# Gate and up products of eight feed-forward turns as two 64-row halves of TensorE's array, the halves changing PSUM banks

## What is computed

```python
h = rms_norm(x, norm2_g[l])
x = x + (jax.nn.silu(h @ w_gate[l]) * (h @ w_up[l])) @ w_down[l]
```

## Time and profile before

| | |
|---|---|
| median of 2 runs | 1517.21 us (1516.51 to 1517.91) |
| profiled execution, its own time | 1516.28 us |
| its span in the profile | 1514.5 us |
| TensorE's mean granted clock in it | 0.998 of full |
| PE, PEld, DVE, ACT busy | 99%, 85%, 71%, 53% of the span |
| DMA | 268.21 MB, mean 177 GB/s |

### The profile page before, as it was taken

How to read it: one execution, slowest core, us unless ns; L and a number is a source line. 1 busy time by engine, 2 the same in 40 slices (tenths; PEclk the granted TensorE clock), 3 DMA queues, 4 the chain that set the end, 5 groups by cost and what they waited for, 6 DMA issues and landing times.

```text
span 1514.5 us, 19707 instructions
## 1 busy us (share of the span) xinstructions
PE 1504.1 (99%) x8062; PEld 1281.8 (85%) x8062; DVE 1072.1 (71%) x1354; ACT 798.4 (53%) x950; POOL 46.6 (3%) x52
## 2 busy tenths in 40 slices
PE   9999999999999999999999999999999999999997
PEld 7888888888888888888888888888888888888886
DVE  5778666676786666885767786666877657876666
ACT  6646444456464444665445364444665455454444
POOL 0100000001000000000300100000002000000000
PEclk9999999999999999999999999999999999999999
DMA  9534545554346555445344455554535445455551
GB/s 295 218 111 174 216 179 200 185 188 167 109 171 217 173 198 181 162 177 175 142 158 165 169 194 197 193 193 174 183 120 197 146 165 181 167 209 194 191 198 56
DMA packets 47802, 268.21 MB, mean 177 GB/s; under 512 B 8288, under 2 KB 11744, under 8 KB 17888
## 3 DMA queue, kind: packets, MB, share of 16 engines
q1 hardware_dynamic: 44960, 264.92, 49.4%
q10 hardware_dynamic: 2752, 2.03, 0.4%
HBM read 262.99 MB, written 1.05 MB: 174 GB/s over the span
## 4 chain that ended last, share of the span: by engine, by line
PE 99%; DVE 0%; DMA 0%; SPq 0%; issue 0%; DVEq 0%; ACT 0%
PE psum L670 21%; PE psum L574 19%; PE psum L576 19%; PE psum L575 19%; PE psum L679 11%; PE psum L612 4%; PE psum L981 1%; PE psum L999 1%; PE psum L1066 1%; PE psum L1075 1%; PE psum L840 0%; PE psum L824 0%; PE psum L988 0%; DMA x<-in_x 0%; PE psum L1053 0%; PE psum L843 0%
## 5 line engine op out<-in xcount | busy, mean ns | idle before, releaser
L1596 DVE TENSOR_TENSOR wl<-raw,wh 128x2048 fp32r<-128x2048 f32 (+1 forms) x247 | 554.7, 2248 | 221.2 <-ACT wh L1176 221.1
L1176 ACT ACTIVATE wh<-raw 128x2048 fp32r<-128x2048 f32 (+2 forms) x249 | 465.9, 1874 | 323.1 <-PE psum L576 200.5
L574 PE MATMUL psum<-wh,xhl 128*128 128x512 f32 (+2 forms) x928 | 365.6, 394 | 0.0
L576 PE MATMUL psum<-wh,xhl 128*128 128x512 f32 (+2 forms) x928 | 357.9, 386 | 0.0
L575 PE MATMUL psum<-wl,xhl 128*128 128x512 f32 (+2 forms) x928 | 357.2, 385 | 0.0
L670 PE MATMUL psum<-xhl,wh 128*128 128x512 f32 x1408 | 336.7, 391 | 0.0
L670 PEld LDWEIGHTS psum<-xhl,wh 128*128 128x128 f32 x1408 | 261.3, 188 | 52.3
L574 PEld LDWEIGHTS psum<-wh,xhl 128*128 128x128 f32 x928 | 174.9, 188 | 34.9 <-issue 2.5
L576 PEld LDWEIGHTS psum<-wh,xhl 128*128 128x128 f32 x928 | 174.6, 188 | 34.7
L575 PEld LDWEIGHTS psum<-wl,xhl 128*128 128x128 f32 x928 | 175.1, 189 | 31.9
L679 PEld LDWEIGHTS psum<-xhl,wl 128*128 128x128 f32 x1408 | 175.3, 192 | 3.8
(11 more groups left out here) (208 smaller groups left out, 1185.9 us busy)
## 6 DMA issues: line engine op xcount, KB each, us to landing
raw<-in_weights SPq DMA_DIRECT2D x233, 1024.0 KB, 4.8
raw<-in_weights SPq DMA_DIRECT2D x10, 512.0 KB, 3.7
raw<-in_weights SPq DMA_DIRECT2D x4, 832.0 KB, 4.3
raw<-in_weights SPq DMA_DIRECT2D x12, 256.0 KB, 8.1
raw<-in_weights SPq DMA_DIRECT2D x2, 768.0 KB, 4.1
arena<-arena SPq DMA_DIRECT2D x8, 192.0 KB, 4.6
work<-in_rpb ACTq DMA_DIRECT2D x8, 141.0 KB, 5.7
arena<-work SPq DMA_DIRECT2D x16, 64.0 KB
```

What stands on the lines that cost most here:

```text
L574: nc.tensor.matmul(dst, lh, right(wh, slot), start=start, stop=False)
L576: return nc.tensor.matmul(dst, ll, right(wh, slot), start=False, stop=stop)
L1176: nc.scalar.activation(wh[:, slot, 0:n], raw[:, slot, 0:n], ACT.Copy).then_inc(high_ready.sem, 1)
L1596: nc.vector.tensor_tensor(wl[:, slot, 0:n], raw[:, slot, 0:n], wh[:, slot, 0:n].bitcast(F32), ALU.subtract).then_inc(split_ready.sem, 1)
```

## The change

Turns 2 to 9 call `gate_up_in_rows` in place of `gate_up` (turn 1 and turn 10 keep the old form). Each stationary tile of 128 rows is cut into rows 0 to 63 and rows 64 to 127, and each moving tile likewise, so a product becomes two of 64 rows, issued one after the other. The two halves write two neighbouring banks: in one run of 8 matmuls the lower half works for group `first` and the upper half for group `first + 1`, and in the `swapped` run the other way round, so that each bank gets both halves. Before a half goes to a bank that the other half has written, PE waits for the end of that run by a new semaphore, `turned`, which the last matmul of the run raises. There are eight such waits and eight such signals in a turn. The sums, the banks, the pieces and the programs of ACT, DVE and SP stay as they are.

```diff
+    "turned": (8 * (FFI - 3), 8 * (FFI - 3)), "aq_ready": (0, 1), "ak_ready": (0, 1), "bv_in": (0, 64),
...
+                def gate_up_in_rows(i, q, slot):
+                    n = 8 * (i - 2)
+                    def run(first, swapped, k0, slot, wide):
+                        for kk in range(4):
+                            for half in range(2):
+                                rows = slice(64 * half, 64 * half + 64)
+                                c = first + (half ^ swapped)
+                                place = bank((up_banks(i) if c >= 2 else gate_banks(i)) + c % 2)
+                                right = slice(kk * 512 + c * P, kk * 512 + (c + 1) * P)
+                                if wide:
+                                    mm = nc.tensor.matmul(place, wh[rows, slot, right],
+                                                          xhl[rows, k0 + kk, :, :].rearrange("p a b -> p (a b)"),
+                                                          start=(k0, kk, swapped) == (0, 0, 0),
+                                                          stop=(k0, kk, swapped) == (4, 3, 0), skip_group_check=True)
+                                else:
+                                    mm = nc.tensor.matmul(place[:, 0:SEQ], wl[rows, slot, right], xh[rows, k0 + kk, :],
+                                                          start=False, stop=False, skip_group_check=True)
+                        return mm
+
+                    pe.wait_ge(*split_ready.by(L, q + 1))
+                    for first in (0, 2):
+                        pe.wait_ge(*proj_free[first // 2].by(L, U + i))
+                        run(first, 0, 0, slot, True).then_inc(turned.sem, 1)
+                    for first in (0, 2):
+                        pe.wait_ge(*turned.by(L, n + 1 + first // 2))
+                        run(first, 1, 0, slot, True)
+                    for first in (0, 2):
+                        run(first, 1, 0, slot, False).then_inc(turned.sem, 1)
+                    for first in (0, 2):
+                        pe.wait_ge(*turned.by(L, n + 3 + first // 2))
+                        mm = run(first, 0, 0, slot, False)
+                    mm.then_inc(piece_used.sem, 1)
+
+                    slot = (slot + 1) % RING
+                    pe.wait_ge(*split_ready.by(L, q + 2))
+                    for first in (0, 2):
+                        run(first, 0, 4, slot, False).then_inc(turned.sem, 1)
+                    for first in (0, 2):
+                        pe.wait_ge(*turned.by(L, n + 5 + first // 2))
+                        run(first, 1, 4, slot, False)
+                    for first in (0, 2):
+                        run(first, 1, 4, slot, True).then_inc(turned.sem, 1)
+                    for first in (0, 2):
+                        pe.wait_ge(*turned.by(L, n + 7 + first // 2))
+                        run(first, 0, 4, slot, True).then_inc(piece_used.sem if first else proj_full[0].sem, 1)
...
                 def turn(i, q, start):
-                    gate_up(i, q, (F + 2) % RING)
+                    (gate_up if start else gate_up_in_rows)(i, q, (F + 2) % RING)
                     down(i - 1, q + 2, (F + 4) % RING, start)
```

More of the change, by code:

```diff
@@ L100 @@
     "a_ready": (11, 11), "ah_ready": (11, 11), "al_ready": (11, 11), "end_ready": (1, 1), "end_high": (1, 1), "end_low": (1, 1), "diag_ready": (1, 1), "row_full": (1, 1), "row_ready": (1, 1),
-    "aq_ready": (0, 1), "ak_ready": (0, 1), "bv_in": (0, 64),
+    "turned": (8 * (FFI - 3), 8 * (FFI - 3)), "aq_ready": (0, 1), "ak_ready": (0, 1), "bv_in": (0, 64),
     "s_full": (0, len(TURNS)), "max_ready": (0, len(TURNS)), "p_ready": (0, len(TURNS)),
@@ L322, in build @@
         s_full, max_ready, p_ready = S["s_full"], S["max_ready"], S["p_ready"]
-        unit_ready, bv_in = S["unit_ready"], S["bv_in"]
+        unit_ready, bv_in, turned = S["unit_ready"], S["bv_in"], S["turned"]
         o_full, o_free = S["o_full"], S["o_free"]
```

## The result

The changed kernel takes 1532.1 us (1531.8 and 1532.4) against 1517.21 before: a ratio of 1.0102, 95% interval 1.0086 to 1.0118, so it is slower by 14.9 us, clear of noise and inside 2%. The forecast was 1530.0, in a range of 1506 to 1546. The profiled execution after took 1532.4 us with a span of 1530.7, 16.1 us over that of before in time and 16.2 in span.

What follows compares the result with a forecast made beforehand. The prediction took TensorE (PE), busy 99% of the span, as the bound. Parts of 0 + 12.8 + 0 + 0 us on the profiled 1516.28 gave 1529.1, or 1530.0 against the median, in a range of 1506 to 1546.

Steps and rivals of the forecast that it cites:

- Part 1: Gate and up products of turns 2 to 9: a pair of 64-row halves costs what one full product costs, 0 us.
- Part 2: 64 changes of the array's shape, into 64-row form and back for `down` each turn, at 0.20 us: +12.8 us.
- Part 3: The eight waits on `turned` a turn are covered by the run of four pairs between: 0 us, upper end 13.
- Part 4: Later gate-bank signals, weight splits on ACT and DVE, and extra instruction fetches all stay hidden elsewhere: 0 us.
- Rival A: Halves shed the float32r products' overhead, wide 0.216 and narrow 0.112 us: faster, 1510.5 us; chance 0.33.
- Rival B: Waits on `turned` bite: the array runs empty at every narrow wait, 25.6 us, 1555.6 us (1581 with wide); chance 0.13.
- Rival C: Float32r halves don't overlap, so each pair costs twice: +355 us, 1885 us; chance 0.03.

Runs made afterwards that it cites:

- the quarters: The changed kernel with four groups of 32 rows in place of two halves, each with its own bank, no waits on `turned`: 1531.66 us, ratio 1.0098.
- the kernel with bare waits: The changed kernel with each wait on `turned` right behind the run it waits for, no other run between: 1617.78 us, ratio 1.0667.

## Why the prediction was right

- **Part 1, pair against product: 0 us, right.** Narrow 3.83 us for 32 and wide 3.65 for 16, before and after. The rows it rested on were plain float32, where a pair kept its product's pace; float32r does the same. In the trace after, the second half starts 0.003 us after the first rather than 0.007, and that doesn't add up over the pairs. This was the disputed step, the one that could have turned the sign, and the quarters say the same once more. The reason I gave, that each row of SBUF is read for the same moving and weight columns, is not shown by this: the runs with fewer weight columns fit it for narrow products only.
- **Part 2, changes of shape: 12.8 us, measured 14.9 to 16.1.** The mechanism and the count were right, the size was low. I priced a change at 0.20 us from the gap and the bare load, and both came out so: 0.09 + 0.11. What I left out is the tail: after a change, wide products run at 0.23 to 0.235 us for some dozen products before they are back at 0.227, another 0.05. The changes in the trace of before could not have told its size: behind the one in rows 7 two products are 0.232 and 0.231 apart, then the pace is 0.227 again, 0.01 in all. But it had the same unevenness without any change of shape, where wide products follow narrow ones: the 16 behind them take 3.65 us, the first 16 of a turn 3.63.

```profile
224.49 3.63 PE psum L670 x16
...
231.95 3.65 PE psum L670 x16
```

  So the tail is not special to a change of shape, and its cause stays open. With the tail 64 x 0.25 = 16.0; the turns of the trace say 15.8, the profiled executions 16.1. The medians differ by 14.9, and the lower bound of the ratio is 13.0 us, so the 12.8 lies just outside the interval.
- **The Trainium skill** ("TensorEngine Tiling (Array Packing)", "Key Properties") says that a change of tiling mode drains TensorE, while a change of tile inside a mode does not. The trace agrees as far as it goes: 0.35 us of idle weight queue at each change of mode, and no seam between runs of pairs inside one. It doesn't show a complete drain: the first load behind the change begins at 226.68, 0.07 before the end that the profile models for the last matmul (226.36 + 0.39).
- **Part 3, waits: 0 us, right**, shown by taking them away (0.2 us of difference). Its working was right as well: exposed, a wait costs 0.335 us where the same terms gave 0.35.
- **Part 4, what hides elsewhere: 0 us, right.** The up banks are free when L1811 (L1763 before) ends, and the next turn begins at 226.68:

```profile
220.20 0.60 ACT L1272 ACTIVATE work<-psum 128x512 f32<-128x512 f32 x1 [2.69 <-PE psum L726]
...
223.56 0.68 DVE L1811 TENSOR_TENSOR work<-psum,work 128x512 f32<-128x512 f32 x1
```

  The read-out waits for the gate banks 2.69 us instead of 1.78, the 0.9 us that the forecast had for the later signal, and the last of it, the up banks, still ends 2.4 us before the next turn.
- **Rival A (faster)** fell with the pace of the pairs. By the rule of the Trainium skill that I set beside it ("TensorE: Matmul & The Clock Gate", Part 3, "The mechanism"), weight loads overlap matmuls only across row groups, and from that I drew that halves should gain. The pairs gained nothing, which fits with the load being beside the matmul already on all 128 rows; the same section also lets a load run ahead if it goes to the background weight buffer, and I had left that out. The rival's floor of 0.111 us was a little high as well: L612 in the trace of before has 128 columns moving and as many loaded at 0.109, which would move its price by 2 us.
- **Rival B** needs an exposed wait, which the change has not. **Rival C** fell with the pairs too: two float32r halves, and even four quarters, run fully beside each other into banks of their own.

## What to carry to other kernels

Cutting a product that fills all 128 rows into row groups gave nothing back here: the groups ran at the pace of the full product (0.227 and 0.120 us), so the only terms left were the changes of shape (here 0.25 us each way) and the waits. Where row groups are wanted for short contractions, put their products together so that the array's form changes rarely. Where two groups must change banks, put a run of other banks between signal and wait; the shortest run here, four narrow pairs or 0.48 us, covered the wait, and that was worth 0.335 us each time.

## What the hardware showed that I had not expected

- After a change of shape wide float32r products run some 2% slower (0.231 for 0.227 us on the mean) for about a dozen products, then fall back into pace by themselves. Wide ones behind narrow ones do so too, by 0.03 us in all, with no change of shape; narrow ones behind a change don't.
- PE takes its own signal quickly: in the kernel with bare waits the signalling run ends at 230.00 and the load that waits for it starts at 230.07, 0.07 us later, against the 0.09 of ACT in rows 10 (both from the modelled end of a matmul).
- A change in the number of stationary columns alone, 128 to 96 and back, makes no seam.
- Fewer stationary columns make narrow products faster and wide ones slower, by up to 0.006 us each at 80 of 128 columns; the sum over a turn is nearly nothing.
